# Landing places of their own for the first adaLN pieces, router logits inside the last projection block, high parts gathered first, and eleven filler matmuls

## What is computed

```python
mod = silu(c) @ ada_w + ada_b                      # adaLN: 1024 x 6144
sh_a, sc_a, gt_a, sh_f, sc_f, gt_f = split(mod, 6)
u = modulate(rms_norm(x, norm_mix_g), sh_a, sc_a)
x = x + gt_a * mixer(u)      # w_in, conv, mLSTM, window attention, two branch projections, w_out
u = modulate(rms_norm(x, norm_ffn_g), sh_f, sc_f)
scores = sigmoid(u @ router_w)                     # top 2 of 16 experts, within one of 4 groups
for e in range(16):
    out += combine[:, e] * ((silu(u @ w_gate[e]) * (u @ w_up[e])) @ w_down[e])
return rms_norm(x + gt_f * out, final_norm_g)
```

## Time and profile before

| | |
|---|---|
| profiled execution, time | 639.07 us |
| its span | 637.3 us |
| TensorE (PE) busy | 593.4 us, 93% |
| VectorE (DVE) busy | 326.7 us, 51% |
| ScalarE (ACT) busy | 225.2 us, 35% |
| DMA | 184.78 MB, mean 290 GB/s |

### The profile page before, as it was taken

The page is one execution under the profiler, slowest core; times in us unless marked ns, Lnnn a source line. Parts: engine busy times, 40 slices in busy tenths (PEclk is TensorE's granted clock), DMA queues, the critical chain, the costliest instruction groups (busy, mean ns, idle before and its releaser), DMA issues.

```text
span 637.3 us, 8441 instructions
## 1 busy us (share of the span) xinstructions
PE 593.4 (93%) x3581; PEld 444.7 (70%) x3581; DVE 326.7 (51%) x515; ACT 225.2 (35%) x300; POOL 5.6 (1%) x13
## 2 busy tenths in 40 slices
PE   4697999999999999999999999889999999998783
PEld 4697988999998888999999886533543533533231
DVE  3895986775758977787454655302212112120103
ACT  3424658544454365665552443201111111110103
POOL 3000000000000000000000000000000000000000
PEclk9997999999999999999999997799999999999997
DMA  8996454877767867725699699199999999999981
GB/s 314 358 359 229 143 194 133 283 259 242 255 216 264 319 214 261 258 77 195 198 338 344 219 374 388 48 398 387 401 387 402 386 401 387 401 387 401 387 325 67
DMA packets 86313, 184.78 MB, mean 290 GB/s; under 512 B 5401, under 2 KB 5505, under 8 KB 86273
## 3 DMA queue, kind: packets, MB, share of 16 engines
q1 hardware_dynamic: 83746, 184.06, 79.9%
q10 hardware_dynamic: 2528, 0.16, 0.3%
HBM read 183.16 MB, written 1.05 MB: 289 GB/s over the span
## 4 chain that ended last, share of the span: by engine, by line
PE 85%; DMA 8%; DVE 3%; ACT 1%; issue 1%; SPq 1%; DVEq 0%; ACTq 0%
PE ps L1287 32%; PE ps L1295 15%; PE ps L1495 14%; PE ps L1506 7%; DMA ring<-in_w_down_e_dram 3%; PE ps L1485 2%; DMA ring<-in_w_gate_e_dram 2%; DMA ring<-in_w_up_e_dram 2%; PE ps L1529 2%; DMA raw<-in_ada_w_dram 1%; PE ps L1235 1%; PE ps L1358 1%; PE ps L1382 1%; PE ps L1397 1%; PE ps L1244 1%
## 5 line engine op out<-in xcount | busy, mean ns | idle before, releaser
L1287 PE MATMUL ps<-u_hi,hi 128*128 128x256 f32 x448 | 130.8, 292 | 9.3 <-DVE u_lo L815 9.3
L755 DVE TENSOR_TENSOR lo<-raw,hi 128x2048 fp32r<-128x2048 f32 x52 | 118.7, 2289 | 35.6 <-ACT hi L514 35.3
L1287 PE MATMUL ps<-u_lo,hi 128*128 128x256 f32 x448 | 128.7, 287 | 0.0
L1287 PE MATMUL ps<-u_hi,lo 128*128 128x256 f32 x448 | 128.6, 287 | 0.0
L1495 PE MATMUL ps<-ring,xe_t 128*64 128x512 f32 x512 | 113.8, 594 | 7.9 <-DMA ring<-in_w_up_e_dram 4.4
L514 ACT CAST hi<-raw 128x2048 fp32r<-128x2048 f32 x52 | 98.8, 1907 | 50.0 <-PE ps L1287 24.8
L1287 PEld LDWEIGHTS ps<-u_hi,hi 128*128 128x128 f32 x448 | 88.0, 196 | 9.6 <-DVE u_lo L815 9.5
L1495 PEld LDWEIGHTS ps<-ring,xe_t 128*64 128x64 f32 x512 | 37.1, 137 | 76.0 <-issue 75.7
L1287 PEld LDWEIGHTS ps<-u_lo,hi 128*128 128x128 f32 x448 | 88.0, 197 | 0.1
L1287 PEld LDWEIGHTS ps<-u_hi,lo 128*128 128x128 f32 x448 | 87.9, 196 | 0.0
L1506 PE MATMUL ps<-ring,he_t 128*64 128x512 f32 x256 | 57.1, 596 | 1.5 <-DMA ring<-in_w_down_e_dram 0.8
(11 more groups left out here) (276 smaller groups left out, 797.0 us busy)
## 6 DMA issues: line engine op xcount, KB each, us to landing
raw<-in_w_in_dram SPq DMA_DIRECT2D x42, 1024.0 KB, 5.3
ring<-in_w_gate_e_dram SPq DMA_DIRECT2D x32, 1024.0 KB, 14.6
ring<-in_w_up_e_dram SPq DMA_DIRECT2D x32, 1024.0 KB, 14.2
ring<-in_w_down_e_dram SPq DMA_DIRECT2D x32, 1024.0 KB, 14.6
raw<-in_ada_w_dram SPq DMA_DIRECT2D x24, 1024.0 KB, 5.5
raw<-in_w_branch_m_dram SPq DMA_DIRECT2D x4, 1024.0 KB, 5.5
raw<-in_w_out_dram SPq DMA_DIRECT2D x4, 1024.0 KB, 7.5
raw<-in_w_branch_a_dram SPq DMA_DIRECT2D x2, 1024.0 KB, 6.4
```

What stands on the lines that cost most here:

```text
L755: V.tensor_tensor(lo[b % RING][:], src[:], hi[b % RING][:].bitcast(F32), ALU.subtract).then_inc(lo_ready, 1)
L1287: ins = mm(dst, w[:, k, cols], x[:, k0 + k, :], start=(first and c % 2 == 0 and k == 0 and n == 0), stop=(end and k == KB - 1 and n == 2), ...
```

## The change

- The first eight adaLN pieces get landing places of their own (`first_ada`) and are cut another way: a piece is two DMAs of one k-tile each with 512 columns of shift and of scale. VectorE takes all eight, two operations of 1024 columns a piece; the piece through TensorE is gone. SP issues pieces and the first four weight blocks without waiting for used places; piece 6 waits for the squares of x and piece 7 for its transposes, whose memory they take.
- x is normalised on ScalarE. Block 0 is split before x_t is copied; u of the first half is split k-tile by k-tile, and block 0 runs k outermost.
- TensorE transposes the small rows first and runs two matmuls of the identity on x ahead of the transposes of x. The column sums of the second half stand in the middle of block 2. The gate weights `w_if` are split at block 6.
- The sixteen later adaLN pieces are one k-tile of 2048 columns each: one VectorE operation instead of four.
- In the last block, the logits of the first half of x stand behind t = 0, and the transposes of tile 0 after k = 1 of t = 1.
- Eight filler matmuls stand behind `start_sums` and three behind the rank sums; their results are used by nothing. The gather takes all high parts first, then the low parts; `xg_lo` is made after the one-hot table.
- In the expert loop, the four matmuls of one chunk stand together and then those of the other; waits and release (`chunk_used`) go by chunk.
- The ring gets a place at 176 KiB (fifth) and loses the one at 120 KiB (last); `xg_hi` and `result` move to 120 KiB.

```diff
-STREAM = ([("ada", a) for a in (0, 1, 4, 5)] + [("w", 0), ("w", 1), ("ada", 2), ("ada", 3), ("w", 2)]
-          + [("ada", 6), ("ada", 7), ("w", 3)])
+FIRST = ([("ada", a) for a in range(4)] + [("w", 0), ("w", 1), ("ada", 4), ("ada", 5), ("w", 2), ("ada", 6), ("ada", 7),
+                                           ("w", 3)])
+STREAM = [item for item in FIRST if item[0] == "w"]
 for _s in range(2, NBLK):
...
-        acc_a = at("acc_a", 120, [P, 2 * D])
+        acc_a = at("acc_a", 120, [P, 2, D])
+        first_ada = [at(f"first_ada{a}", k, [P, 2, 2, NB]) for a, k in enumerate((96, 104, 112, 144, 48, 72, 164, 156))]
...
         ring = [at(f"ring{i}", k, [P, KB * FF]) for i, k in enumerate(
-            [140, 148, 192, 96, 80, 88] + last_raw[0:2] + [112, 104] + last_raw[2:4]
+            [140, 148, 192, 96, 176, 80, 88] + last_raw[0:2] + [112, 104] + last_raw[2:4]
             + [32 + 8 * ((NBLK - 3) % RING), 56 + 8 * ((NBLK - 3) % RING), 32 + 8 * ((NBLK - 2) % RING),
-               56 + 8 * ((NBLK - 2) % RING), 32 + 8 * ((NBLK - 1) % RING), 56 + 8 * ((NBLK - 1) % RING), 120])]
+               56 + 8 * ((NBLK - 2) % RING), 32 + 8 * ((NBLK - 1) % RING), 56 + 8 * ((NBLK - 1) % RING)])]
...
+            ada_first = A["ada_w"][0].rearrange("(p k) (m n) -> p k m n", k=KT, m=6)
+            for kind, n in FIRST:
+                if kind == "w":
+                    sp.dma_start(raw[n][:], block_source((kind, n))).then_inc(raw_loaded[n], 16)
+                else:
+                    if n == 6:
+                        after(sp, "x_ss")
+                    if n == 7:
+                        after(sp, "x_t")
+                    j, k = n // KB, 2 * (n % KB)
+                    for i in range(2):
+                        sp.dma_start(first_ada[n][:, i], ada_first[:, k + i, 0:2, j * NB:(j + 1) * NB]
+                                     ).then_inc(ada_landed[n], 16)
             for n, item in enumerate(STREAM):
-                if n >= RAW:
-                    used_up(sp, STREAM[n - RAW])
+                if n < RAW:
+                    continue
+                used_up(sp, STREAM[n - RAW])
...
-                    sp.wait_ge(block_done, NBLK - 8 + n // 2)
+                if n in (11, 12):
+                    used_up(sp, ("w", NBLK - 13 + n))
+                if n in (13, 15, 17):
+                    sp.wait_ge(block_done, NBLK - 2 + (n - 13) // 2)
                 load_chunk(n)
             after(sp, "logits")
             sp.dma_start(fin_g[:], A["final_norm_g"].rearrange("(a n) -> a n", a=1).broadcast_to([P, D])).then_inc(fin_loaded, 16)
             for n in range(RSLOTS, CHUNKS):
-                sp.wait_ge(group_used, (n - RSLOTS) // 2 + 1)
+                sp.wait_ge(chunk_used, n - RSLOTS + 1)
                 load_chunk(n)
...
+            after(act, "x_rms")
+            for t in range(TT):
+                ins = A_(x_in[:, t, :], x_in[:, t, :], ACT.Copy, scale=st[:, 6 + t:7 + t])
+            event(ins, "x_norm")
...
+            split_hi(0)
             after(act, "x_t")
...
-            split_hi(0)
-            u_split_hi(0)
+            after(act, "x_up", "chan0")
+            for k in range(KB):
+                event(A_(u_hi[:, k, :], x_t[:, k, :], ACT.Identity, scale=chan[:, 2, k:k + 1], bias=chan[:, 0, k:k + 1]),
+                      f"u_hi0_{k}")
             split_hi(1)
...
+                if a < ADA_FIRST:
+                    j = a // KB
+                    dve.wait_ge(ada_landed[a], 32)
+                    dst = acc_a[:, :, j * NB:(j + 1) * NB]
+                    if a % KB:
+                        dve.wait_ge(ada_done, a)
+                    for i in range(2):
+                        kk = 2 * (a % KB) + i
+                        if kk == 0:
+                            step(V.tensor_scalar(dst, first_ada[a][:, i], cs[:, 0:1], None, ALU.mult))
+                            continue
+                        ins = V.scalar_tensor_tensor(out=dst, in0=first_ada[a][:, i], scalar=cs[:, kk:kk + 1], in1=dst,
+                                                     op0=ALU.mult, op1=ALU.add)
+                        if i == 0:
+                            step(ins)
+                    ins.then_inc(ada_done, 1)
+                    return
...
+                if k:
+                    dve.wait_ge(ada_done, a)
+                dst = mod[:, 2 * h:2 * h + 2, :].rearrange("p m n -> p (m n)")
+                V.scalar_tensor_tensor(out=dst, in0=src[:].rearrange("p k n -> p (k n)"), scalar=cs[:, k:k + 1], in1=dst,
+                                       op0=ALU.mult, op1=ALU.add).then_inc(ada_done, 1)
...
-            ada(1)
+            for a in range(4):
+                ada(a)
+                if a == 0:
+                    after(dve, "vec_t")
+                    event(V.tensor_copy(vec[:], ps[0][:, 0:104]), "vec")
+            split_lo(0)
+            modulate(0, 1)
+            split_first()
+            split_lo(1)
             ada(4)
             ada(5)
-            modulate(0, 1)
-            split_lo(0)
-            u_split_lo(0)
-            split_lo(1)
-            ada(2)
-            ada(3)
 
...
-            for t in range(TT):
-                after(dve, f"xg_hi{t}")
-                V.scalar_tensor_tensor(out=xg_lo[:, t, :], in0=x_res[:, t, :], scalar=st[:, 14 + t:15 + t],
-                                       in1=xg_hi[:, t, :].bitcast(F32), op0=ALU.mult, op1=ALU.subtract).then_inc(xg_split, 1)
-
...
             build_onehot(0)
+            for t in range(TT):
+                after(dve, f"xg_hi{t}")
+                V.scalar_tensor_tensor(out=xg_lo[:, t, :], in0=x_res[:, t, :], scalar=st[:, 14 + t:15 + t],
+                                       in1=xg_hi[:, t, :].bitcast(F32), op0=ALU.mult, op1=ALU.subtract).then_inc(xg_split, 1)
...
+            def mod_columns(j, bank):
+
+                pe.wait_ge(ada_done, 4 * (j + 1))
+                for m in range(2):
+                    for c in range(KB):
+                        n = KT * m + KB * j + c
+                        ins = mm(ps[bank][:, n:n + 1], acc_a[:, m, (KB * j + c) * P:(KB * j + c + 1) * P], ones[:, 0:1],
+                                 start=(m == 0 and c == 0), stop=True, skip_group_check=True)
+                event(ins, f"mod_col{j}")
+
+            pe.wait_ge(rows_loaded, 80)
+            event(tr(ps[0][:, 0:104], rows[0:104, :], ident[0:104, 0:104]), "vec_t")
             after(pe, "x_norm")
+            for n in range(2):
+                mm(ps[2 + n][:], ident[:], x_in[:, 0, 0:NB], start=True, stop=True)
             for k in range(KT):
                 for t in range(TT):
                     ins = tr(ps[4 + k // 2][:, (k % 2) * T + t * P:(k % 2) * T + (t + 1) * P],
                              x_in[:, t, k * P:(k + 1) * P], ident[:])
             event(ins, "x_t")
-            pe.wait_ge(rows_loaded, 80)
-            event(tr(ps[0][:, 0:104], rows[0:104, :], ident[0:104, 0:104]), "vec_t")
-            mod_columns(0, 0, 1)
-            mod_columns(0, 1, 1)
+            mod_columns(0, 1)
...
+                if s == 0:
+
+                    for k in range(KB):
+                        after(pe, f"u_lo0_{k}")
+                        for c in range(4):
+                            dst = ps[banks[c // 2]][:, (c % 2) * T:(c % 2 + 1) * T]
+                            cols = slice(c * P, (c + 1) * P)
+                            for n, (w, x) in enumerate(((w_hi, x_hi), (w_hi, x_lo), (w_lo, x_hi))):
+                                ins = mm(dst, w[:, k, cols], x[:, k, :], start=(c % 2 == 0 and k == 0 and n == 0), stop=False,
+                                         skip_group_check=True)
+                elif channel_major:
                     for c in range(4):
+                        if s == EARLY - 1 and c == 2:
+                            after(pe, "x_up")
+                            mod_columns(1, 7)
                         dst = ps[banks[c // 2]][:, (c % 2) * T:(c % 2 + 1) * T]
...
+                            if s == NBLK - 1 and t == 1 and k == 1:
+                                after(pe, "x1_1_t0")
+                                for c in range(KB):
+                                    tr_ins = tr(ps[6][:, c * P:(c + 1) * P], x_res[:, 0, NB + c * P:NB + (c + 1) * P], ident[:])
+                                event(tr_ins, "x1_turn1_t0")
                         if s == NBLK - 1 and t == 0:
                             event(ins, "wo_t0")
+                            after(pe, "x1_turned0", "mod3")
+                            logits(0, 0)
+                            logits(1, 0)
...
+            after(pe, "x1_turned1_t0")
+            logits(0, 1)
+            after(pe, "x1_1_t1")
+            for k in range(KB):
+                ins = tr(ps[7][:, k * P:(k + 1) * P], x_res[:, 1, NB + k * P:NB + (k + 1) * P], ident[:])
+            event(ins, "x1_turn1_t1")
+            after(pe, "x1_turned1_t1")
+            event(logits(1, 1), "logits")
...
+            def keep_busy(n):
+
```

(45 more changed lines are left out.)

166 lines of the change are left out of this document (52 added, 114 removed).

## The result

The changed kernel takes 655.03 us (median of 4 runs, 653.53 to 655.12) against 638.39 for the kernel before in the same session (4 runs, 637.15 to 639.4): ratio 1.026, 95% interval 1.023 to 1.028. I forecast 630.4 and faster. It is slower by 16.6 us.

What follows compares the result with a forecast made beforehand. It took the expert part as bound by DMA at 2.71 us a chunk. The terms -4.1 - 1.8 + 0.6 - 1.9 = -7.2 gave a 630.1 us span; the forecast was 630.4 us, range 625.5 to 635.0.

Steps and rivals of the forecast that it cites:

- Start, -1.0 and -4.1: Before the block matmuls: block 0 starts 1.0 us earlier, the fourth block 4.1 us earlier, the 1.0 included.
- Clock behind the hole, -1.8: After TensorE's wait before the fourth block: a shorter wait avoids the slow-clock stretch, saving 1.8 us.
- End of the mixer, +0.6: Last block to the router's logits: mostly the same work in changed places, 0.6 us longer.
- Logits to experts, -1.9: Router's logits to first expert matmul: xg_lo leaves the path before the ranks and the gather runs faster, 1.9 us saved.
- I take it that it still reaches over them: 0: Expert loop: despite four matmuls of each expert in a row, both array halves still work at once; cost 0.
- the sign named for this case: Expert part: single weight loads every 0.43 us and DMA share below 1 would show the forecast wrong.
- serial halves: Expert loop: one array half's four matmuls run before the other's; price about +110 us, chance 0.14.
- rival 1: Expert loop: the slower rival, serial halves, about 745 to 786 us; chance 0.14.
- The point from which it decides: Expert loop: TensorE binds instead of DMA once a chunk costs it over 2.3 us.
- the sum's -7.2: Whole kernel: the terms together take 7.2 us off the 637.3 us span, giving 630.1.

Runs made afterwards that it cites:

- by twos: The alternating kernel with the two experts' matmuls ordered 0,0,1,1,0,0,1,1 inside a chunk pair: 633.05 us, ratio 0.990.
- The threes: The alternating kernel with the two experts' matmuls ordered 0,0,0,1,1,1,0,1 inside a chunk pair: 636.89 us, ratio 0.998.
- The alternating kernel: The changed kernel with the old matmul order 0,1,0,1 inside a chunk pair, waiting for both chunks: 632.51 us, second time 631.6.

## Why the prediction was wrong

**Start, -1.0 and -4.1: right.** Block 0 starts at 27.27 (27.4 put), the fourth block at 49.88 (50.0 put). The chain was the one worked out: the column sums of the second half stand between the halves of block 2 (L1268 from 43.93 to 45.85), VectorE is through with block 3's split at 45.99, and it and ScalarE need until 49.8. The 14.03 us for the first 96 matmuls stand in no row (the earlier trace rows has 14.32); TensorE did not bind there, so it changed nothing.

**Clock behind the hole, -1.8: right.** The hole is 1.04 us (0.9 put), and the 240 records after it take 29.06 instead of 30.82; from 50 to 52 us, just behind it, the granted clock is 1.00 where it was 0.50 behind the old hole.

**End of the mixer, +0.6: right.** From the last block's first half (376.53) to the sums it takes 8.9 us, 9.0 put. **Logits to experts, -1.9: right in kind, measured -2.8** (13.96 instead of 16.72). The four sums took 5.2 us instead of 6.2 in this execution, the clock not being at its low level throughout. That 1 us is the luck of the outcome: by twos, with the sums at 5.93, the stretch takes 14.7, against 14.8 put, and the logits ahead of it 0.8 us more. That xg_lo covers the high matmuls is in the chain (394.61 xg_lo, and behind it no more than the low parts).

**"I take it that it still reaches over them: 0": the step that failed.** The term put at 0 is about +23 us. The reasoning was: two records stand together at the head of a group, so TensorE looks past its next instruction; hence it will look past sixteen as past four. The first half is right and the second is an extrapolation from one distance to a fourfold one, which no row of before could carry. In the old order the records ahead of the other half's first number two, one of them under way. The rows showed a reach of one and left open everything beyond. The runs put it at three records not yet started, and the sign named for this case came: single weight loads every 0.43 us, and a DMA share of 0.88 instead of 1.01 at the end.

**The bounds of that step were wrong too.** I let it be 0 or serial halves (+110 us), and put 0.14 on the latter. Serial halves did not come: rival 1 had the side and not the mechanism. The loss lies at the ends of a run of chunks, not in each chunk. What the rule of the Trainium skill, page "TensorE: Matmul & The Clock Gate", section "Part 3: Packing small matmuls — row/col tiling" (matmuls start and end in program order), would give is about 745 us and more; measured are 655. The trace speaks against its strict form, since the second expert's first record starts at 401.15 and three of the first expert's only after it, one every 0.43 us; a reach that ends after three records is nearer to it than my own assumption was.

**The point from which it decides was wrong as well.** I wrote that TensorE may take up to 2.3 us a chunk before it binds. With 3.95 us more a pair it takes 1.755 + 3.95 / 12 = 2.08, and the kernel still lost 23 us in its experts. The 2.71 us a chunk of DMA holds for 77 chunks, but TensorE has 96 to work through, 19 of them loaded beforehand. The right comparison is over the whole stage. There the room was already in the earlier trace rows: TensorE waits for nothing until 560 us, and idles 60 - 51.36 = 8.6 us between 560 and 620. That is about all it could lose for free, 1.1 us a pair. Eight pairs by 3.95 are 31.6, less 8.6 leaves 23.0, and 23 is what the order costs. By the chain both terms are somewhat larger. Without its waits for landings the old loop would end 10 us before 623.56 (two pairs at 24.14 and a group of 7.02 behind 558.21); the order adds 33.5 (3.8 up to the first down group, seven times 3.95, and 1.9 in the last group). The difference is 23.5 again. The threes fit as well: 8 x 1.77 = 14.2, less 8.6 is 5.6, and their experts take 221.3 us where the alternating ones take 615.3 - 399.5 = 215.8, 5.5 less.

**With that one step put right the rest of the sum stands, nearly.** The alternating kernel has the sum's -7.2 in it and nothing of the order: its two profiled spans are 629.8 and 628.3, with 630.1 put; its medians lie 5.5 and 6.5 us below the kernel before in their sessions, 0.7 to 1.7 short of the 7.2. The last scatter at the lower clock (0.7) is a term that the sum did not have, and the outcomes at the four sums make up to 3 us. Taking the alternating kernel as the base, the order costs 655.0 - 632.5 = 22.5 us (653.3 - 629.8 = 23.5 between two spans with the same outcome), and on the kernel before 661.0 - 638.0 = 23.

The best versions measured all have the alternating order: without the eleven fillers 0.988 of the kernel before (0.987 to 0.990), with them split 2 and 9 0.989 (0.987 to 0.990, twice). These runs do not tell the two apart.

## What to carry to other kernels

When two column halves of the array work side by side, interleave their matmuls so that no more than four records of one half stand in a row (two matmuls here, since each float32 one is two records). Four matmuls of 512 columns in a row cost 1.77 us for each uninterrupted run of chunks between two stretches of full-width work. The order 0,0,1,1 loses nothing that these runs show (633.05 against 632.51 and 631.6 us).

Before you put 0 on a reordering, add up the engine's idle time over the whole stage, since that is about all the slack it has (8.6 us here, 10 by the chain), and read the number of instructions in a stretch beside its busy time: busy 79.8 of 80 us stood for 406 records before and 340 after. And a behaviour seen at one distance (here: the next instruction but one) is evidence for that distance.
